# Difference attention in a two-block transformer: the two softmaxes of a head are combined before the turn, not after the values

## The reference, cut to what matters

```python
qa = split_heads(qa, 2 * DIFF_HEADS)          # 8 query/key units of 64
ka = split_heads(ka, 2 * DIFF_HEADS)
va = jnp.repeat(split_heads(va, DIFF_HEADS), 2, axis=1)   # both units of a head share v
o = causal_block_attention(qa, ka, va, HEAD_DIM ** -0.5)  # softmax(q k^T) v
o = o.reshape(B, DIFF_HEADS, 2, S, DIFF_V)
o_a = o[:, :, 0] - lam * o[:, :, 1]           # lam: one number per layer
o_a = merge_heads(rmsnorm(o_a, subln_g) * (1.0 - lam_init))
```

## Time and profile before

| | us |
|---|---|
| median of three runs | 1952.64 |
| span of the profiled execution | 1949.7 |
| TensorE busy in it | 1913.1 (98%) |
| VectorE busy | 1532.6 (79%) |
| ScalarE busy | 1256.1 (64%) |
| attention1, layer 0 (first scores to last values) | 39.8 to about 121 |
| attention1, layer 1 | 392 to about 475 |

### The profile page before, as it was taken

One profiled execution on the slowest core, in us unless ns is written; L12 is line 12 of the kernel. 1 busy time (PEld: TensorE's weight loads), 2 busy tenths in 40 slices (PEclk: granted clock), 3 DMA queues, 4 the chain that ended last, 5 costly groups with the idle time before them and its releaser, 6 DMA issues.

```text
span 1949.7 us, 27758 instructions
## 1 busy us (share of the span) xinstructions
PE 1913.1 (98%) x10275; PEld 1628.8 (84%) x10275; DVE 1532.6 (79%) x1814; ACT 1256.1 (64%) x1668; POOL 38.6 (2%) x28
## 2 busy tenths in 40 slices
PE   8999999999899999999999999999999999999998
PEld 7879998888688888888888888888887798888987
DVE  5575555657789989898998989999897865877586
ACT  5654535555777778777887877878777556354542
POOL 0000000000000000000000000000120000000000
PEclk9999999999999999999999999999999999999999
DMA  7717555430899999999999999999996452345320
GB/s 248 249 52 263 182 186 173 152 130 27 319 359 390 362 394 360 394 366 390 392 360 392 360 396 387 362 390 361 396 369 227 158 178 95 123 160 194 130 96 36
DMA packets 246214, 514.64 MB, mean 264 GB/s; under 512 B 12517, under 2 KB 59241, under 8 KB 246121
## 3 DMA queue, kind: packets, MB, share of 16 engines
q1 hardware_dynamic: 242936, 502.77, 71.7%
q0 software_dynamic: 2896, 10.49, 1.3%
q10 hardware_dynamic: 288, 0.11, 0.0%
HBM read 507.56 MB, written 5.77 MB: 263 GB/s over the span
## 4 chain that ended last, share of the span: by engine, by line
PE 84%; DVE 10%; ACT 3%; issue 1%; DMA 1%; ACTq 0%; DVEq 0%
PE bank L756 26%; PE bank L758 25%; PE bank L757 25%; DVE low L1993 3%; DVE low L2593 2%; PE bank L1178 1%; PE bank L727 1%; ACT high L1456 1%; PE bank L880 1%; DMA scr<-expert_rows,kept_row 1%; DVE at L2804 1%; PE bank L871 1%; PE bank L849 1%; DVE kT L2829 0%; DVE qT L2828 0%
## 5 line engine op out<-in xcount | busy, mean ns | idle before, releaser
L2593 DVE TENSOR_TENSOR low<-raw,high 128x1024 fp32r<-128x1024 f32 x672 | 783.5, 1219 | 73.0 <-ACT high L1660 71.5
L1660 ACT ACTIVATE high<-raw 128x1024 fp32r<-128x1024 f32 x336 | 357.2, 1063 | 206.4 <-PE bank L758 205.0
L1993 DVE TENSOR_TENSOR low<-raw,high 128x2048 fp32r<-128x2048 f32 (+1 forms) x138 | 310.4, 2259 | 163.9 <-ACT high L1456 163.5
L1456 ACT ACTIVATE high<-raw 128x2048 fp32r<-128x2048 f32 (+1 forms) x138 | 260.8, 1895 | 165.6 <-PE bank L758 153.9
L756 PE MATMUL bank<-high,xg_hi 128*128 128x512 f32 x896 | 353.6, 395 | 1.2 <-DVE xg_lo L2573 1.2
L1661 ACT ACTIVATE high<-raw 128x1024 fp32r<-128x1024 f32 x336 | 351.7, 1047 | 0.0
L758 PE MATMUL bank<-high,xg_lo 128*128 128x512 f32 x896 | 349.4, 390 | 0.0
L757 PE MATMUL bank<-low,xg_hi 128*128 128x512 f32 x896 | 348.8, 389 | 0.0
L756 PE MATMUL bank<-high,xT_hi 128*128 128x512 f32 (+1 forms) x576 | 227.3, 395 | 3.5 <-DVE xT_lo L2015 1.3
L758 PE MATMUL bank<-high,xT_lo 128*128 128x512 f32 (+1 forms) x576 | 221.4, 384 | 0.0
L757 PE MATMUL bank<-low,xT_hi 128*128 128x512 f32 (+1 forms) x576 | 221.2, 384 | 0.0
(11 more groups left out here) (349 smaller groups left out, 2345.7 us busy)
## 6 DMA issues: line engine op xcount, KB each, us to landing
raw<-in_moe_w_gate SPq DMA_DIRECT2D x112, 1024.0 KB, 7.8
raw<-in_moe_w_up SPq DMA_DIRECT2D x112, 1024.0 KB, 8.3
raw<-in_moe_w_down SPq DMA_DIRECT2D x112, 1024.0 KB, 8.2
raw<-in_w_in SPq DMA_DIRECT2D x63, 1024.0 KB, 5.2
raw<-in_w_out SPq DMA_DIRECT2D x20, 1024.0 KB, 4.9
raw<-in_dense_w_gate SPq DMA_DIRECT2D x11, 1024.0 KB, 5.4
raw<-in_dense_w_up SPq DMA_DIRECT2D x11, 1024.0 KB, 5.4
raw<-in_dense_w_down SPq DMA_DIRECT2D x11, 1024.0 KB, 5.0
```

Of the source, the lines that this page charges most:

```text
L1456: act.activation(high[:, slot, 0:k * n], raw[:, raw_slot[piece], 0:k * n], ACT.Copy).then_inc(high_done, 1)
L1660: act.activation(part[:, 0:HALF // 2], raw[:, slot, 0:HALF // 2], ACT.Copy).then_inc(s["high_half"], 1)
L1993: dve.tensor_tensor(low[:, slot, 0:k * n], src, high[:, slot, 0:k * n].bitcast(F32), ALU.subtract).then_inc(low_done, 1)
L2593: last = dve.tensor_tensor(low_part[:, cols], raw[:, at0 + k % slots, cols], high_part[:, cols].bitcast(F32), ALU.subtract)
```

## The change

VectorE combines the two probability tiles of a head in SBUF, before anything is turned. Then one tile a head is turned, copied and multiplied with the values. The waits of `exps`, `copy_turned`, `turn` and `values` count turned tiles (`turn_first`) and no longer units; for fox and in the second block the order stays as it was. The steps in which M and E of the second unit of a pair are issued move from i+1 to i. Head hd is turned in step 2hd+1 and multiplied in step 2hd+2. `setup_lambda` moves ahead of the first `mix_pair`. The `diff_out` that is left only copies.

```diff
+            def turn_pair(l, p):
+                pe.wait_ge(pair_mixed, 4 * l + p + 1)
+                turn_probs("diff", turn_first["diff", l] + p, probs[:, 0, :])
...
# TensorE, attention1
-                    if 0 <= i - 1 < len(RUN1):
-                        turn(RUN1[i - 1][0], first + i - 1)
+                    if i in (1, 3, 5, 7):
+                        turn_pair(l, i // 2)
+                    if 9 <= i <= 12:
+                        turn("fox", first + i - 1, units + i - 9)
...
-                        values(name, u, first + i - 2)
+                    if i in (2, 4, 6, 8):
+                        hd = i // 2 - 1
...
+                        values("diff", 2 * hd, heads + hd)
...
# ScalarE
-            def exps(name, u, g):
+            def exps(name, u, g, turned):
                 act.wait_ge(att_max, g + 1)
-                if g >= 2:
-                    act.wait_ge(att_turned, g - 1)
+                if turned > 0:
+                    act.wait_ge(att_turned, turned)
...
-                    if i < len(RUN1):
-                        exps(*RUN1[i], first + i)
+                    if i < 8 and i % 2 == 0:
+                        exps("diff", i, first + i, heads + i // 2)
+                        exps("diff", i + 1, first + i + 1, heads + i // 2)
+                    if (l, i) == (0, 0):
+                        serve(stat[:, 1, 0:2 * LAYERS], stat[:, 0, 0:2 * LAYERS], ACT.Exp)
+                    if 8 <= i < 12:
+                        exps("fox", i - 8, first + i, units + max(0, i - 9))
...
-                    if i >= 1:
-                        copy_turned(RUN1[i - 1][0], first + i - 1)
+                    if i in (1, 3, 5, 7):
+                        copy_turned("diff", heads + i // 2)
+                    if i >= 9:
+                        copy_turned("fox", units + i - 9)
...
# VectorE
+                def mix_pair(hd):
+                    dve.wait_ge(att_exp, first + 2 * hd + 2)
                     r = rinv[:, 4 * hd:4 * hd + 4]
                     link(dve.reciprocal(r, rowsum[:, 4 * hd:4 * hd + 4]))
                     link(dve.tensor_scalar(r[:, 2:4], r[:, 2:4], lam[:, l:l + 1], None, ALU.mult))
...
+                    for t, (c0, n) in enumerate(spans):
+                        last = dve.tensor_scalar(probs[:, 1, c0:c0 + n], probs[:, 1, c0:c0 + n], r[:, 2 + t:3 + t], None,
+                                                 ALU.mult)
+                    link(last)
+                    for t, (c0, n) in enumerate(spans):
+                        last = dve.scalar_tensor_tensor(out=probs[:, 0, c0:c0 + n], in0=probs[:, 0, c0:c0 + n],
+                                                        scalar=r[:, t:t + 1], in1=probs[:, 1, c0:c0 + n], op0=ALU.mult,
+                                                        op1=ALU.add)
+                    last.then_inc(pair_mixed, 1)
+                def diff_out(hd):
+                    dve.wait_ge(att_pv, heads + hd + 1)
+                    dve.tensor_copy(ya[:, :, hd, :], bank[4 + hd % 2][:, 0:SEQ].rearrange("p (t d) -> p t d", t=NT)).then_inc(
+                        out_taken, 1)
...
-                    maxima(*RUN1[i], first + i)
+                    if i < 8 and i % 2 == 0:
+                        maxima(*RUN1[i], first + i)
+                        maxima(*RUN1[i + 1], first + i + 1)
+                    if (l, i) == (0, 0):
+                        setup_lambda()
+                    if i in (1, 3, 5, 7):
+                        mix_pair(i // 2)
+                    if i >= 8:
+                        maxima(*RUN1[i], first + i)
                     if i in (3, 5, 7, 9):
                         diff_out((i - 3) // 2)
...
                     if 1 <= i <= 8:
                         splits(pieces_of[("va", "vfb", "qkb", "qkc", "vgc")[(i - 1) // 2], l][(i - 1) % 2])
-                    if (l, i) == (0, 1):
-                        setup_lambda()
```

More of the change, by code:

```diff
@@ L505, in program @@
         att_first, att_n, out_use = {}, 0, {}
+        turn_first, turn_n = {}, 0
         for l in range(LAYERS):
-            for name, n in (("diff", 8), ("fox", 4)):
+            for name, n, turns in (("diff", 8, 4), ("fox", 4, 4)):
                 att_first[name, l], att_n = att_n, att_n + n
+                turn_first[name, l], turn_n = turn_n, turn_n + turns
             for k in range(4):
@@ L886, in attention1 @@
                 first = att_first["diff", l]
+                heads, units = turn_first["diff", l], turn_first["fox", l]
                 rows_half([("va", l, t) for t in range(NT)], ("va", l), 0, (0,))
@@ L907, in attention1 @@
                         last.then_inc(unit_full, 1)
-                    if i >= 2:
-                        name, u = RUN1[i - 2]
-                        if (name, u) == ("diff", 0):
+                    if i in (2, 4, 6, 8):
+                        hd = i // 2 - 1
+                        if hd == 0:
                             emptied(pe, ("va", l, 1))
[L912 to L916, removed]
+                        pe.wait_ge(out_taken, out_use["diff", l, max(0, hd - 1)])
+                        if hd == 2:
+                            emptied(pe, ("forgetT", l))
+                        values("diff", 2 * hd, heads + hd)
+                    if i >= 10:
+                        if i == 10:
                             pe.wait_ge(out_taken, out_use["diff", l, 3])
-                        values(name, u, first + i - 2)
+                        values("fox", i - 10, units + i - 10)
                     if i < 10:
@@ L955, in attention2 @@
             def attention2(l):
-                first = att_first["moba", l]
+                first, units = att_first["moba", l], turn_first["moba", l]
                 emptied(pe, ("kaT2", l, 1))
@@ L967, in attention2 @@
                     if 0 <= i - 1 < len(RUN2):
-                        turn(RUN2[i - 1][0], first + i - 1)
+                        turn(RUN2[i - 1][0], first + i - 1, units + i - 1)
                     if i >= 2:
@@ L976, in attention2 @@
                             pe.wait_ge(out_taken, out_use["memory", l, 0])
-                        values(name, u, first + i - 2)
+                        values(name, u, units + i - 2)
                     if i < 4:
@@ L1030, in mixed @@
                 output(l, 1, 0)
-                pe.wait_ge(att_copied, att_first["fox", l] + 4)
+                pe.wait_ge(att_copied, turn_first["fox", l] + 4)
                 output(l, 0, 1)
@@ L2187, in attention1 @@
                 ya = y1[:, :, 0:512].rearrange("p t (h n) -> p t h n", h=4)
-                def diff_out(hd):
-                    dve.wait_ge(att_pv, first + 2 * hd + 2)
+                heads = turn_first["diff", l]
+                def mix_pair(hd):
+                    dve.wait_ge(att_exp, first + 2 * hd + 2)
                     r = rinv[:, 4 * hd:4 * hd + 4]
@@ L2195, in diff_out @@
                     link(dve.tensor_scalar(r[:, 2:4], r[:, 2:4], lam[:, l:l + 1], None, ALU.mult))
[L2196 to L2201 removed]
+                    spans = att_shape("diff")[2]
+                    for t, (c0, n) in enumerate(spans):
[11 more added lines that the diff above has]
+                        out_taken, 1)
                 for i in range(len(RUN1)):
@@ L2262, in attention1 @@
                 turned_y(l, 1)
-                dve.wait_ge(att_pv, first + len(RUN1))
+                dve.wait_ge(att_pv, turn_first["fox", l] + 4)
                 link(dve.reciprocal(rinv[:, 0:8], rowsum[:, 0:8]))
```

55 lines of the change are left out of this document (26 added, 29 removed).

## The result

The changed kernel takes 1988.97 us (median of five runs, 1988.02 to 1990.98) against 1952.64 us (1949.26 to 1954.53) of the kernel before in the same rounds: a ratio of 1.0198, 95% interval 1.0187 to 1.0209. It is slower: the two medians are 36 us apart, the ratio makes it 39. The forecast was 1984.

The account below looks back on a forecast made before the run. TensorE, busy 98% of the span, was taken as the bound. Waits less savings and tail gave +24.8 us, the clock 7: +31.8, span 1949.7 to 1981, median 1984; range 1973 to 1994.

Parts of the forecast that it names:

- What mix_pair costs: On VectorE, reciprocal and lambda product, two tensor_scalar and two scalar_tensor_tensor take 1.75 us a head, bounds 1.3 and 2.3.
- The added wait: TensorE's turn_pair waits for mix_pair, queued behind the previous step's L, which waits for ScalarE's H; 17.0 us in layer 1.
- The covers: Time TensorE has work from S to T's place: 3.91, 5.12, 7.5 and 7.5 us for heads 0 to 3.
- What TensorE saves: One T and one V go per head, 0.92 us; 3.7 us a layer, 7.4 us in all.
- The tail: At the attention's end, shorter diff_out in step 9 pulls fox exps forward; step 12's 1.09 us wait mostly goes: 1.1 us a layer.
- The clock: TensorE's new waits bring four to five falls to about half clock, 1.6 us each: 7 us.
- My two bounds: Limits of the clock term: 0 and 8 x 1.6 = 13 us.
- the signs: Wrong if turns wait under about 2 us, layer 0's attention is not about 12 us longer, or clock stays 1.00.
- that only the saving counts: Rival at turn_pair: half projections cover the mixing, nothing waits; 1943 us, chance 0.04.
- That the clock stays: Rival: TensorE's waits come without falls of the clock; 1977 us, chance 0.24 shared with something given back.
- that the loss is given back later: Rival: loads run ahead while TensorE waits, 3 to 8 us return; 1976 to 1981, chance 0.24 shared with no falls.
- the rival with a worse chain: Cumulative sum or takes slip into each other, or more than one half-speed stretch a wait; 1990 to 2000, chance 0.11.

Follow-up runs that it names:

- x1: Changed kernel with mix_pair one step earlier on VectorE, behind the two M and ahead of that step's splits; 1955.54 us, ratio 1.0027 to the kernel before.
- x6: Changed kernel with a head's T, C and V one step later and the previous head's diff_out ahead of mix_pair; 1945.82 us, ratio 0.9977 to the kernel before.
- x2: Changed kernel with TensorE given products that nothing reads ahead of each T of a head; 1976.77 us, ratio 1.014 to the kernel before.
- x9: x6 with the last head's diff_out and diff_sums in step 9 ahead of M and E of the second fox unit; 1942.82 us, ratio 0.996.
- x4: Changed kernel without the arithmetic of mix_pair, which only waits for both E and signals at the same place; 1971.82 us, ratio 1.0098.

## Why the prediction was right, and where its sizes were off

The mechanism was as forecast, and its working can be held against the rows one by one.

*What mix_pair costs.* 1.75 us forecast; from the end of L to the start of T 1.86 (layer 0, head 1: 59.73 to 61.59). From start to start the two pairs of instructions take 0.58 and 0.67 us, forecast 0.6 and 0.68; the 0.1 us over is the way from the last one to T.

*The added wait.* From S to T's release, forecast and measured in layer 1: head 0 5.5 and 5.6 us; head 1 9.4 and 9.5; head 2 14.25 and 14.2; head 3 11.5 and 11.5. The covers: 3.91 and 4.1, 5.12 and 5.3, 7.5 and 7.7, 7.5 and 7.45. The waits: 1.6, 4.3, 6.7, 4.0 forecast; 1.52, 4.18, 6.44, 4.02 measured, and in layer 0 2.4 forecast for head 0 and 2.19 measured. Together with V's wait (0.4 a layer forecast, 0.23 measured) 34.8 against 33.5 us. x1 shows that the order L, then mixing, is the cause of it.

*What TensorE saves.* 7.4 us forecast, and it is there: the T and V are gone. In x6 the two stretches are 6.1 us shorter though T and V wait for 2.8 in them; less the old stalls of 0.6, that puts the saving near 8. The prediction's sentence that TensorE has no gap in steps 0 to 8 was not quite right: those two stalls for `kT` were there, and it counted them at 0.2 us a layer.

*The tail.* Forecast was 1.1 us a layer from the wait of step 12. This step failed. The rotation does end earlier against the second fox S, but M of the second fox unit then waits for its scores, and the fox exps are no earlier against the turns: the 1.09 us stand unchanged (the row at 132.95 above, and the same at 504.77), and they stand in x6 too. The earlier rotation gave something else: from second fox S to last V layer 0 takes 14.81 us instead of 15.63. At layer 1's end there went besides the clock fall of 467.3 to 470.6 (14.82 instead of 17.16). All in all the stretches outside the two attentions gave 3.3 us, none of it by the wait that the forecast's 2.2 us were to come from.

*The clock.* 7 us forecast, 17.3 as the remainder above, 15.8 by x2: the mis-sized term, and more than the whole of the distance from 1981 to 1989.2. Two numbers in it were too small. The falls were seven and not four to five, with one behind the 2.19 us wait of head 0 in layer 0, which I had put among the short ones. And each cost 2.3 to 2.5 us on average and not 1.6: I had taken the length of a fall, 3.3 us, from the rows of before, where they follow waits of 1 to 2 us, and six of these seven lasted 6.8 us or longer. By the rule of the Trainium skill that the prediction cited (TensorE: Matmul & The Clock Gate, "Why this matters for your kernels") the six long waits pay; the trace agrees for all six, and a seventh, shorter one paid as well. My two bounds, 0 and 13 us, did not hold the value: eight times the old price is no upper end where the price was read behind shorter waits.

The sum: 34.8 - 7.4 - 0.4 - 2.2 + 7.0 = 31.8 forecast; 33.5 - 7.4 - 0.6 - 3.3 + 17.3 = 39.5 in the profile, with the 7.4 taken over and the 17.3 as what is left. The forecast is 8 us short of the span and only 5 short of the median, and that is luck: the profiled run was the slowest of its five, so the median lies 0.2 us below the span and not 2.9 above it. One of the signs that it gave for being wrong came up as well: layer 0's attention, from first S to last V, was to be about 12 us longer and is 21.3 (79.9 to 101.3). Waits and savings alone come to about 12 there; the sign left out the clock term that the forecast itself added.

The rivals: that only the saving counts was the furthest off, and x6 and x9 show what it takes, which is another place for three calls. That the clock stays was refuted by the seven windows, that the loss is given back later by 1.3 us more, not less, behind the router. Of the rival with a worse chain the chains held to a tenth or two, but its other half came, in kind: six of the falls lasted 6.8 us or more where 3.3 was counted.

## What to carry to other kernels

Before moving work to another engine, write down what stands ahead of it in that engine's queue, and what that waits for: here 1.9 us of arithmetic a head cost 36 us because it stood behind a split that waited for a third engine, and one call moved gave most of it back. When a consumer is put later to cover a chain, look at every other thing that is queued behind the same instruction; a short copy that others wait for goes ahead of a longer step that nobody needs yet. And price a wait of TensorE at more than its length: here 33 us of waiting brought 12 to 17 us of half speed with it.

## What the runs showed of the hardware

In the changed kernel a wait of TensorE of 1.52 us (layer 1, head 0) brought no fall of the clock, one of 2.19 us (layer 0, head 0) did, and so did all six of 4.0 to 6.5 us. Between them length alone does not decide: in x4 a wait of 2.36 us in layer 1 went with a fall and one of 2.37 us in layer 0 did not, and in x1 one of 1.84 us did in layer 0 (72.2 to 75.6) and its like in layer 1 did not. Behind the long waits TensorE did 4.5 to 5.8 us of work at 1.2 GHz before the clock was back. At half clock three transposes took 0.90 us instead of 0.55. Falls also come and go where nothing in the code near them differs: the 1.09 us wait of the fox turn was followed by a fall in layer 1 and not in layer 0 in the kernel before, and in x6 it is the other way about (112.0 to 115.4). Each of the eleven profiles has one or two more between 494 and 557 us, in the stretch of small instructions at the router. The 33 runs of the kernel before lie between 1947.64 and 1955.2 us, with mean granted clocks of 0.999 at the lower end and 0.995 to 0.997 at the upper, which is why differences of 3 us needed some ten runs each.
